# Inverse roots of the norms as Exp of half the negative logarithm on ScalarE, and a last norm that reads and stores in place

## The reference, cut to what matters

```python
def _rms(x):
    return x * lax.rsqrt(jnp.mean(x * x, axis=-1, keepdims=True) + 1e-6)

def _modulate(x, shift, scale):
    return _rms(x) * (1 + scale) + shift

def _layer_norm(x, g, b):            # 1e-6 in the first block, 1e-5 in the second
    mu = jnp.mean(x, axis=-1, keepdims=True)
    var = jnp.mean(jnp.square(x - mu), axis=-1, keepdims=True)
    return (x - mu) * lax.rsqrt(var + EPS) * g + b
```

## Time and profile before

| what | value |
|---|---|
| median of three runs | 2791.62 us (2791.62 to 2791.8) |
| profiled execution, first to last instruction (its span) | 2782.0 us |
| TensorE busy | 2667.0 us, 96% |
| VectorE busy | 1925.3 us, 69% |
| ScalarE busy | 1517.7 us, 55% |
| read from memory | 578.82 MB, 208 GB/s over the span |

### The profile page before, as it was taken

The page is one execution under the profiler, slowest core; times in us unless marked ns, Lnnn a source line. Parts: engine busy times, 40 slices in busy tenths (PEclk is TensorE's granted clock), DMA queues, the critical chain, the costliest instruction groups (busy, mean ns, idle before and its releaser), DMA issues.

```text
span 2782.0 us, 39479 instructions
## 1 busy us (share of the span) xinstructions
PE 2667.0 (96%) x14416; PEld 2189.5 (79%) x14416; DVE 1925.3 (69%) x2538; ACT 1517.7 (55%) x2202; POOL 18.1 (1%) x20
## 2 busy tenths in 40 slices
PE   7998999999998999989999999999999999999997
PEld 3764778888655899869999867888888888888886
DVE  2676655543267676575555655789898988989896
ACT  3233442322355544355444354678787877878784
POOL 0000000000000000000001000000000000000000
PEclk9998999999999999999999989999999999999999
DMA  6656122222220445324553312599999989989893
GB/s 257 242 225 274 61 91 93 104 91 91 91 76 31 147 172 182 122 76 147 185 184 137 121 61 106 199 350 379 346 370 352 367 350 350 364 343 376 348 364 136
DMA packets 80644, 581.53 MB, mean 209 GB/s; under 512 B 8848, under 2 KB 10128, under 8 KB 10128
## 3 DMA queue, kind: packets, MB, share of 16 engines
q1 hardware_dynamic: 80528, 579.90, 55.4%
HBM read 578.82 MB, written 1.05 MB: 208 GB/s over the span
## 4 chain that ended last, share of the span: by engine, by line
PE 85%; DVE 8%; ACT 3%; DMA 2%; issue 1%; POOL 0%; SPq 0%; ACTq 0%; DVEq 0%
PE ps L2482 7%; PE ps L2484 7%; PE ps L2483 7%; PE ps L289 7%; PE ps L290 7%; PE ps L291 7%; PE ps L2509 4%; PE ps L2511 4%; PE ps L2510 4%; PE ps L1114 3%; PE ps L1112 3%; PE ps L1113 3%; DVE parts L264 2%; DMA ring<-in_stream_dram 2%; PE ps L396 1%; PE ps L308 1%
## 5 line engine op out<-in xcount | busy, mean ns | idle before, releaser
L264 DVE TENSOR_TENSOR parts<-ring,parts 128x1024 fp32r<-128x1024 f32 x294 | 357.4, 1224 | 407.0 <-ACT parts L255 394.8
L255 ACT ACTIVATE parts<-ring 128x1024 fp32r<-128x1024 f32 x294 | 307.7, 1054 | 456.7 <-PE ps L291 196.2
L289 PE MATMUL ps<-parts 128*128 128x256 f32 (+1 forms) x1472 | 474.9, 323 | 8.6 <-DVE arena L1184 5.4
L290 PE MATMUL ps<-parts 128*128 128x256 f32 (+1 forms) x1472 | 470.0, 319 | 0.0
L291 PE MATMUL ps<-parts 128*128 128x256 f32 (+1 forms) x1472 | 469.6, 319 | 0.0
L2707 DVE TENSOR_TENSOR parts<-ring,parts 128x1024 fp32r<-128x1024 f32 x280 | 331.8, 1218 | 12.0 <-ACT parts L2549 0.3
L2549 ACT ACTIVATE parts<-ring 128x1024 fp32r<-128x1024 f32 x280 | 291.9, 1060 | 55.7 <-PE ps L2484 47.3
L289 PEld LDWEIGHTS ps<-parts 128*128 128x128 f32 x1472 | 280.5, 191 | 38.4 <-DVE arena L1184 9.4
L2482 PE MATMUL ps<-parts 128*128 128x512 f32 x752 | 296.8, 395 | 0.5 <-DVE parts L2707 0.5
L290 PEld LDWEIGHTS ps<-parts 128*128 128x128 f32 x1472 | 280.6, 191 | 19.8 <-issue 0.2
L291 PEld LDWEIGHTS ps<-parts 128*128 128x128 f32 x1472 | 280.7, 191 | 19.6
(11 more groups left out here) (414 smaller groups left out, 4745.3 us busy)
## 6 DMA issues: line engine op xcount, KB each, us to landing
ring<-in_stream_dram SPq DMA_DIRECT2D x380, 1024.0 KB, 5.7
h<-in_stream_dram SPq DMA_DIRECT2D x112, 1024.0 KB, 7.1
arena<-in_stream_dram SPq DMA_DIRECT2D x56, 1024.0 KB, 7.1
x<-in_x_dram SPq DMA_DIRECT2D x1, 2048.0 KB, 7.8
tab<-in_table_dram SPq DMA_DIRECT2D x1, 1724.5 KB, 10.1
out_dram<-x SPq DMA_DIRECT2D x1, 1024.0 KB, 4.8
tab<-in_table_dram SPq DMA_DIRECT2D x1, 184.5 KB, 2.7
arena<-in_table_dram SPq DMA_DIRECT2D x1, 144.0 KB, 13.6
```

Source lines behind the costliest of these rows:

```text
L255: nc.scalar.activation(self.w_lead[:, self.buffer(g)], units(ring[:, n % NS, :])[:, g % UPS], ACT.Copy)\
L264: nc.vector.tensor_tensor(self.w_rest[:, self.buffer(g)], units(ring[:, n % NS, :])[:, g % UPS], self.w_lead[:, self.buffer(g)].bitcast(F3 ...
L289: nc.tensor.matmul(dst, wl[:, k, :], xl, start=(k == 0), stop=False)
L290: nc.tensor.matmul(dst, wl[:, k, :], xr, start=False, stop=False)
```

## The change

A function `inverse_root` makes 1/sqrt(a*x + eps) on ScalarE as exp(-0.5 * ln(a*x + eps)), and takes the place of Sqrt and RECIPROCAL in all norms. A table set that holds both functions is loaded by name, at fixed places. The last norm reads the experts' sums where they are, the copies go, and the output is stored in four pieces.

```diff
+    def load_log_exp():
+        nc.scalar.preload_act_table_set("natural_log_exp_and_others")
+
+    def inverse_root(act, dst, logs, src, eps, scale=1.0):
+        act.add(nc.scalar.activation(logs, src, ACT.Ln, scale=scale, bias=col(eps)))
+        act.settle()
+        return nc.scalar.activation(dst, logs, ACT.Exp, scale=-0.5)
```

In `modulate`, and in the same way in `layer_norm`, in the mixer's head norm and convolution norm, and in the eight norms of `mla_proj`:

```diff
-            nc.scalar.activation(std, ps[:, bank, 0:W], ACT.Sqrt, bias=col("eps6")).then_inc(G["std"], 1)
+            inverse_root(act, rstd, std, ps[:, bank, 0:W], "eps6").then_inc(G["std"], 1)
...
             G.wait(dve.eng, "std", 1)
-            dve.add(nc.vector.reciprocal(rstd, std))
-            dve.settle()
```

```diff
                 nc.scalar.activation(sig_o[:, n, :], ps[:, bank, :], ACT.Sigmoid).then_inc(sem("m_sig_o_ready"), 1)
+            load_log_exp()
             eng.wait_ge(sem("m_cols_done"), 1)
             nc.scalar.activation(gcol[:, :, :], ps[:, 3, :].rearrange("p (t r) -> p t r", t=4), ACT.Copy)\
               .then_inc(sem("m_gcol_ready"), 1)
```

The end of the experts, and of the program:

```diff
             def spread(r):
                 eng.wait_ge(S("GT"), r + 1)
-                eng.wait_ge(S("y_dve"), r + 1)
                 for j in range(4):
+                    if j % 2 == 0:
+                        eng.wait_ge(S("y_dve"), r * 2 + (j // 2 + 1))
...
+            hold(5, 0)
             spread(n)
...
-            sums(n)
-            eng.wait_ge(S("sum"), n * 4 + 6)
-            for k in range(KD):
-                nc.vector.tensor_copy(x[:, k, T:NTOK], x[:, k, 0:T]).then_inc(S("x"), 1)
+            sums(n, S("x"))
...
-    add(layer_norm("ln4", moe_ready, 3, (0, 1), alone=True))
+    add(layer_norm("ln4", moe_ready, 3, (0, 1), alone=True, source=slice(0, T)))
...
-            signals[final].wait(sp, "x", KD)
-            sp.dma_start(out, x[:, :, T:NTOK] if upto is None else x[:, :, :]).then_inc(out_stored, 16)
-            sp.wait_ge(out_stored, 16)
+            for k in range(0, KD, 2):
+                signals[final].wait(sp, "x", k + 2)
+                sp.dma_start(out[:, k:k + 2, :], x[:, k:k + 2, T:NTOK] if upto is None else x[:, k:k + 2, :])\
+                  .then_inc(out_stored, 16)
+            sp.wait_ge(out_stored, 16 * KD // 2)
```

More of the change, by code:

```diff
@@ L802, in scalar @@
                         later_row_out(act, m)
-            warm(act, ACT.Sqrt)
             squares_of(act, HEADS_M - 1)
             act.settle()
-            nc.scalar.activation(small[:, 16:32], small[:, 0:16], ACT.Sqrt, scale=1.0 / V_M, bias=col("eps6"))\
+            inverse_root(act, small[:, 40:56], small[:, 16:32], small[:, 0:16], "eps6", 1.0 / V_M)\
               .then_inc(sem("m_rms_ready"), 1)
@@ L812, in scalar @@
             N.wait(eng, "var", 1)
-            nc.scalar.activation(gi, ps[:, 4, :], ACT.Sqrt, bias=col("eps6")).then_inc(N["std"], 1)
+            inverse_root(act, lfs, gi, ps[:, 4, :], "eps6").then_inc(N["std"], 1)
             warm(act, ACT.Silu)
@@ L983, in vector @@
             eng.wait_ge(sem("m_rms_ready"), 1)
-            dve.add(nc.vector.reciprocal(small[:, 0:16], small[:, 16:32]))
-            dve.settle()
             hg = hs.rearrange("p t h v -> p (t h) v")
-            nc.vector.tensor_tensor(hg, hg, small[:, 0:16].rearrange("p (g o) -> p g o", o=1).to_broadcast([P, 16, V_M]),
+            nc.vector.tensor_tensor(hg, hg, small[:, 40:56].rearrange("p (g o) -> p g o", o=1).to_broadcast([P, 16, V_M]),
                                     ALU.mult).then_inc(sem("m_hs_ready"), 1)
@@ L1500, in scalar @@
             act.settle()
-            nc.scalar.activation(st[:, 52:56], st[:, 48:52], ACT.Sqrt, scale=1.0 / KVL, bias=col("eps6"))\
+            inverse_root(act, st[:, 56:60], st[:, 52:56], st[:, 48:52], "eps6", 1.0 / KVL)\
               .then_inc(S("ck_std"), 1)
@@ L1507, in scalar @@
             act.settle()
-            nc.scalar.activation(st[:, 62:64], st[:, 60:62], ACT.Sqrt, scale=1.0 / QL, bias=col("eps6"))\
+            inverse_root(act, st[:, 64:66], st[:, 62:64], st[:, 60:62], "eps6", 1.0 / QL)\
               .then_inc(S("cq_std"), 1)
@@ L1649, in mla_attention, with layer_norm @@
                          mla_turned, ATT_BASE, nxt="mla_out")
-    def layer_norm(name, after, which, banks, feeds=None, alone=False, held=0):
+    def layer_norm(name, after, which, banks, feeds=None, alone=False, held=0, source=slice(T, NTOK)):
         G = Signals("norm", name, added=0 if alone else 5, mean=1, square=KD, var=1, centred=KD, std=1, scaled=KD, x=KD)
@@ L1679, in means @@
                 mm = nc.tensor.matmul(ps[:, banks[0], 0:T], col("over1024"),
-                                      sq[:, 0, :] if k == 5 and not alone else x[:, k, T:NTOK],
+                                      sq[:, 0, :] if k == 5 and not alone else x[:, k, source],
                                       start=(k == (0 if alone else 5)), stop=(k == KD - 1))
@@ L1714, in scalar @@
         def scalar(act):
+            if alone:
+                load_log_exp()
             for k in range(KD):
@@ L1718, in scalar @@
             G.wait(act.eng, "var", 1)
-            nc.scalar.activation(std, ps[:, banks[1], 0:T], ACT.Sqrt, bias=col("eps5")).then_inc(G["std"], 1)
+            inverse_root(act, rstd, std, ps[:, banks[1], 0:T], "eps5").then_inc(G["std"], 1)
             if feeds:
@@ L2686, in outputs, with sums @@
                     eng.wait_ge(S("y_act"), 2 * r + (n + 1))
[L2687 to L2692, removed]
+                    nc.vector.scalar_tensor_tensor(y_rest[:, 512 * n:512 * n + 512], ps[:, 4 + n, :], gcol,
+                                                   y_lead[:, 512 * n:512 * n + 512].bitcast(F32),
+                                                   ALU.mult, ALU.subtract).then_inc(S("y_dve"), 1)
+            def sums(r, signal):
                 eng.wait_ge(S("sum"), r * 4 + 2)
@@ L2697, in sums @@
                     nc.vector.tensor_tensor(acc, ps[:, (6, 7, 4, 5)[j], :].rearrange("p (m t) -> p m t", m=2), acc,
-                                            ALU.add).then_inc(S("sum"), 1)
+                                            ALU.add).then_inc(signal, 1)
             for m in range(2):
@@ L2734, in vector @@
                     if g == 0:
-                        sums(r)
+                        sums(r, S("sum"))
                     else:
```

22 lines of the change are left out of this document (7 added, 15 removed).

## The result

The changed kernel takes 2770.84 us (median of eight runs, 2761.6 to 2781.2), the kernel before 2791.22 (eight runs, 2779.9 to 2795.7). The ratio is 0.9934, with a 95% interval of 0.9917 to 0.995, so 18 us faster. The forecast was 2776.0, in a range of 2771 to 2784. The median lies 0.2 us outside that range.

A forecast was written before the change was run, and what follows sets the result against it. TensorE was taken as the bound, 85% of the chain of waits. Gains of 9.2 us until the experts end and 6.55 behind them, 15.75 together, took the span from 2782.0 to 2766.2; plus 9.6 gave 2776, whole range 2771 to 2784.

The forecast's parts named there:

- gate columns: Table load put ahead of the copy L776, for whose result TensorE waits: a loss of 1.3 us.
- conv norm: Norm ahead of the output projection, where TensorE idles 0.76 us before the first product: +0.6 us (0 to 0.76).
- mla_mod: Norm without a weight cut; TensorE waits 0.56 us for the first piece only, dummies cap the gain: +0.55 us.
- ffn1_mod, ln1, ln2: Three norms on 256 columns: scaling 0.97 us earlier at each, second piece moving in full, +2.9 us together.
- ln3: Norm where TensorE waits 0.50 us, ahead of which the dummies end: +0.45 us.
- router load: Table load before the router's Exp goes, as the log-exp set is in place since ln3: +1.3 us.
- gather, until the first expert product: The gather's 32 products, partly at 1.2 GHz after idle time, expected at 2.4 GHz: +2.3 us (0 to 2.3).
- last spread and means: Program's end: five dummies keep TensorE busy, spread at 0.12 us a product, means follow at once: +3.0 us.
- output: Four stores issued as their pieces are ready, the last moving a quarter: +2.2 us (0 to 2.6).
- from the span to the median: Median run taken as 9.6 us longer than the profiled span, unchanged by the edit: 2766.2 becomes 2775.8 us.
- rival (c): Clock: gather stays slow, 2.3 us, three further stretches fall to 1.2 GHz at 1.7 each: 2783.4 us; chance 0.12.
- rival (a): Dummies cap every norm, later waits don't shrink: 3.0 us less gain, 2779.0 us; chance 0.12.

The follow-up runs named there:

- roots alone: The changed kernel with the end as before (copies, one signal, no dummies ahead of the last spread, one store): 2779.85 us, ratio 0.9965.

## Why the prediction was right, and where it was off

By step, what the traces show against what was forecast, in us:

| step | forecast | measured |
|---|---|---|
| gate columns | -1.3 | -1.4 |
| conv norm | +0.6 | +1.1 |
| ffn0_mod | +2.65 | +2.5 |
| mla_mod | +0.55 | +0.7 |
| MLA query | -0.25 | -0.24 |
| ffn1_mod, ln1, ln2 | +2.9 | +3.0 |
| ln3 | +0.45 | +0.7 |
| router load | +1.3 | +0.3 to +1.7 |
| gather, until the first expert product | +2.3 | +1.9 |
| last spread and means | +3.0 | +3.2 |
| last norm | +1.35 | +1.34 |
| output | +2.2 | +2.3 |

The sum of 15.75 stands: the steps make 15.4 to 16.8. Each is the distance between two events around the edit in the two profiled executions (the upper value at the router is that of roots alone, whose dummies ran at full clock). Three of them hold a change of clock: up to the first product L2436 the gather's row has 2.2 us by it, the spread 1.3, and the router's 0.3 has lost 1.4. Without these some 13 us are left, more than the 10.0 at an equal clock; the 3 us between are not explained. That the median comes out as near as it does is in part luck: at an equal clock less was won than forecast, and the clock's rise made up for it.

The step that failed is the one from the span to the median, "is 9.6 us longer; that lies around the span and stays". Only 1.8 lie around it. The other 7.8 are the profiled execution of before being quicker than its median, in good part by its clock (0.984 as its mean against 0.982 over all runs of before, 4.5 us by the line). The number still served, since the difference of two medians doesn't ask where the 9.6 lies. But with the cause taken for a constant, and three known runs within 0.2 us of each other, I did not see that a median moves by several microseconds with the clock: 2776 missed 2770.8 by 5, mainly through that. The range was too narrow downward for the same reason. A forecast for a kernel whose eight runs span 16 us can't end 5 us under its centre. The clock was in the sum at two places only (2.3 and about 1.7), and as rival (c) only as a loss; over the runs it was a gain of 7.4, if the eight runs are typical.

Rows of idle time give less than an edit can win. Ahead of the conv norm's product, ln3 and mla_mod, the records showed 0.76, 0.50 and 0.56 us of idle, and 1.1, 0.7 and 0.7 were won: a product that follows a dummy at once starts 0.2 to 0.4 us before the end that the record of the dummy gives. That is also why L308 stands at 347.49 behind dummies that end at 347.84 by their record.

At ffn1_mod, ln1 and ln2 the second piece moved in full. At ln1 it stood 6.67 us behind the start of the dummies and stands at 5.68:

```profile
1250.29 4.48 PE L352 MATMUL ps<-tab 128*128 128x256 f32 x20
...
1254.42 0.47 PE L308 MATMUL ps<-parts 128*128 128x256 f32 x1
...
1255.97 0.39 PE L308 MATMUL ps<-parts 128*128 128x256 f32 x1 [0.85 <-DVE parts L273]
```

The first product moved by 0.83 only, up to the dummies, and the second by 0.99, its wait having fallen from 1.12 to 0.85. So rival (a) is out.

The gather's own 2.0 us came near the forecast 2.3. The products behind it are faster by 1.2 too (2.82 to 1.60), but won nothing: the first expert product follows the first of them by a chain of cuts that takes 2.4 us at either clock, and 0.3 more with the table load in it. What was late next behind the gather was not asked. And of the room that the prediction saw in the dummies there, 1.4 us were lost when part of them ran at half clock.

For the output, 2.3 us came where 2.2 were forecast. The fit that the prediction set beside it would have given 1.8; the Trainium skill (DMA: Bandwidth & Descriptors, Anatomy of one DMA) states it for DMAs issued by GpSimd, and these stores are issued by SyncE.

## What to carry to other kernels

Ask of each execution how much of it ran at half clock before explaining a difference of 0.5%; the same instructions moved by 16 us here, and 0.47 us for each microsecond at half clock accounted for all but 2 us of it. When an engine comes earlier, the dummies that covered its wait become the bound: at mla_mod they left 2.0 us of the reciprocal's gain unused. Two functions in turn on ScalarE paid here only with one table set for both (0.9934 against 1.0012).

## What the runs showed of the hardware

A stand of 1.7 us ahead of the gather came with half clock in both executions that had it, one of 1.56 us ahead of the last spread with full clock in the one that had it, and 2.3 us there with half clock in all three. These few executions don't tell what decides. Near the router half clock came, at one place or another, in 13 of the 14 executions, whether its load stood there or not. A table load took 1.28 us in every run. A store of 128, 256 and 1,024 KB landed 1.9, 2.5 and 4.8 us after its issue.
